# Expert calls in which heads 0 and 1 are routed before the first dot, and half of the first v rows is gathered behind the first 32 u

## The reference, cut to what matters

```python
q = (xc @ w_q).reshape(PEER_CHUNK, PEER_HEADS, 2, PEER_HALF)      # 128 tokens, 8 heads
s = jnp.einsum('thid,hikd->thik', q, sub_keys)
s1, i1 = lax.top_k(s[:, :, 0], 16); s2, i2 = lax.top_k(s[:, :, 1], 16)
# the 16 best of the 256 sums s1 + s2 name 16 of 16,384 experts per token and head
u = u_emb[eidx]
hid = jax.nn.gelu(jnp.einsum('td,thkd->thk', xc, u))
return jnp.einsum('thk,thkd->td', gate * hid, v_emb[eidx])
```

## Time and profile before

| | us |
|---|---|
| median of three runs | 3790.22 (3789.51 to 3791.14) |
| span of the profiled execution | 3786.1 |
| first gather of call 1, 2, 3 issued at | 582.9, 1480.4, 2606.9 |
| last gather issued in call 3 | 3287.4 |
| DVE busy in the span | 1978.6 (52%) |
| POOL busy | 1527.8 (40%) |
| PE busy | 3085.9 (82%) |

### The profile page before, as it was taken

How to read it: one execution, slowest core, us unless ns; L and a number is a source line. 1 busy time by engine, 2 the same in 40 slices (tenths; PEclk the granted TensorE clock), 3 DMA queues, 4 the chain that set the end, 5 groups by cost and what they waited for, 6 DMA issues and landing times.

```text
span 3786.1 us, 31001 instructions
## 1 busy us (share of the span) xinstructions
PE 3085.9 (82%) x11474; PEld 1349.7 (36%) x11474; DVE 1978.6 (52%) x4448; ACT 367.0 (10%) x923; POOL 1527.8 (40%) x1579
## 2 busy tenths in 40 slices
PE   7999887778988987688888889888466666798897
PEld 4484445233532325222222224446011111144343
DVE  0051447767776635666666623355777777223132
ACT  1000321110000001000000000131000000012111
POOL 0010004646665662666666641002677777500000
PEclk9999998879999988899999989999889898899999
DMA  6274137979999997999999987416999999942322
GB/s 270 99 292 169 72 128 300 358 252 392 410 408 410 405 385 273 362 412 411 411 412 412 412 344 281 171 68 261 371 409 409 409 407 397 361 164 82 113 89 100
DMA packets 257376, 1125.52 MB, mean 297 GB/s; under 512 B 29636, under 2 KB 34980, under 8 KB 238024
## 3 DMA queue, kind: packets, MB, share of 16 engines
q0 software_dynamic: 221184, 805.40, 54.1%
q1 hardware_dynamic: 32456, 312.82, 21.2%
q10 hardware_dynamic: 3584, 5.31, 0.4%
HBM read 1117.06 MB, written 6.37 MB: 297 GB/s over the span
## 4 chain that ended last, share of the span: by engine, by line
PE 44%; DMA 26%; DVE 17%; POOL 7%; issue 4%; ACT 3%; DVEq 0%; SPq 0%; ACTq 0%; POOLq 0%
DMA big<-in_u,xT 17%; PE ps L234 16%; DMA big<-in_v,xT 7%; POOL big L2132 7%; DVE big L2101 6%; PE ps L1961 5%; PE ps L1900 5%; PE ps L656 4%; PE ps L1399 2%; PE ps L670 1%; PE ps L1517 1%; PE ps L1435 1%; DVE small L910 1%; PE ps L387 1%; PE ps L587 1%
## 5 line engine op out<-in xcount | busy, mean ns | idle before, releaser
L1961 PE MATMUL ps<-big,bc 128*32 128x512 f32 x3072 | 1074.1, 671 | 344.1 <-DMA big<-in_v,xT 330.5
L2101 DVE CUSTOM_DVE_ANT_0 big<-big,ps 128x1024 f32<-128x1024 f32 x768 | 926.5, 1215 | 427.6 <-DMA big<-in_u,xT 423.8
L2132 POOL DMA_INDIRECT big<-in_u,xT x768 | 729.2, 950 | 611.9 <-issue 163.5
L2132 POOL DMA_INDIRECT big<-in_v,xT x768 | 727.8, 948 | 281.6 <-issue 187.1
L234 PE MATMUL ps<-w,xT 128*128 128x512 f32 x1408 | 615.0, 598 | 8.8 <-ACT xT L256 6.0
L1961 PEld LDWEIGHTS ps<-big,bc 128*32 128x32 f32 x3072 | 194.8, 116 | 1102.0 <-DMA big<-in_v,xT 733.6
L234 PEld LDWEIGHTS ps<-w,xT 128*128 128x128 f32 x1408 | 268.4, 192 | 346.6 <-issue 334.0
L524 POOL TENSOR_TENSOR small<-small 128x32 f32<-128x32 f32 (+1 forms) x8 | 33.2, 4154 | 374.4 <-DVE small L495 250.6
L1900 PE MATMUL ps<-tmp,w 128*128 128x256 f32 x768 | 172.5, 387 | 2.0 <-ACT tmp L256 2.0
L656 PE MATMUL ps<-w,xT 128*128 128x512 f32 x384 | 167.1, 594 | 1.7 <-ACT bb L755 0.9
L1900 PEld LDWEIGHTS ps<-tmp,w 128*128 128x128 f32 x768 | 148.7, 195 | 24.0 <-ACT tmp L256 3.2
(11 more groups left out here) (305 smaller groups left out, 2783.4 us busy)
## 6 DMA issues: line engine op xcount, KB each, us to landing
w<-in_w_in SPq DMA_DIRECT2D x58, 2048.0 KB, 9.2
bc<-in_w_mod SPq DMA_DIRECT2D x21, 2048.0 KB, 10.6
w<-in_w_conv SPq DMA_DIRECT2D x24, 1536.0 KB, 9.1
w<-in_peer_wq SPq DMA_DIRECT2D x12, 2048.0 KB, 9.3
w<-in_w_out SPq DMA_DIRECT2D x10, 2048.0 KB, 8.1
w<-in_conv_out_w SPq DMA_DIRECT2D x6, 2048.0 KB, 8.7
big<-in_u,xT POOLq DMA_INDIRECT x768, 10.5
big<-in_v,xT POOLq DMA_INDIRECT x768, 10.8
```

The lines of the kernel that those rows point to most:

```text
L1961: ins = pe.e.matmul(self.ps[32 * g:32 * g + 32, 2 + half, :], p["diag"][part % 2][:, 256 * g + 32 * m:256 * g + 32 * m + 32], p["ring"][:, ...
L2101: dve.inc(dve.e.tensor_tensor_reduce(out=row, in0=row, in1=p["xc"], scale=1.0, scalar=0.0, op0=ALU.mult, op1=ALU.add, accum_out=p["hid"][t ...
L2132: ins = pool.e.indirect_dma_start(p["ring"][:, slot, :], None, table, bass.IndirectOffsetOnAxis(index, 0))
```

## The change

The list becomes u0 to u31, v0 to v15 (positions 32 to 47), then eight times four u and two v (u32 to u35 at 48 to 51, v16, v17, u36 to u39, ...), which ends with u63 at position 93 and v31 at 95. From position 96 on it is as before. DVE routes steps 0 and 1 one after the other ahead of the first dot; PE makes the scores of step 1 behind query 3 and not behind query 5; ACT makes the exponential of step 1 behind query 7 and not behind query 15.

```diff
     def peer_order(self):
-        order = [("u", e) for e in range(PART)]
-        for part in range(PARTS):
+        order = [("u", e) for e in range(PART)] + [("v", e) for e in range(PART // 2)]
+        for i in range(0, PART // 2, 2):
+            order += [("u", PART + 2 * i + j) for j in range(4)]
+            order += [("v", PART // 2 + i + j) for j in range(2)]
+        for part in range(1, PARTS):
...
-        for i in range(2, 6):
+        for i in range(2, 4):
             query(i)
         scores(1)
-        for i in range(6, 16):
+        for i in range(4, 16):
             query(i)
...
-            if i == 3:
-                self.gate_exp_act(act, name, p, 0)
+            if i in (3, 7):
+                self.gate_exp_act(act, name, p, i // 4)
...
-                if e % TOPK == 11 and e // TOPK + 1 < STEPS:
+                if e % TOPK == 11 and 1 < e // TOPK + 1 < STEPS:
...
-        alone(self.route_dve(dve, l, name, p, 0))
+        for step in range(2):
+            alone(self.route_dve(dve, l, name, p, step))
...
-                routing = self.route_dve(dve, l, name, p, step + 1) if step + 1 < STEPS else iter(())
+                routing = self.route_dve(dve, l, name, p, step + 1) if 1 < step + 1 < STEPS else iter(())
```

## The result

The changed kernel takes 3803.8 us (median of 14 runs, 3795.5 to 3808.8), the kernel before 3793.0 on the same chip (14 runs). The ratio is 1.0026, 95% interval 1.0018 to 1.0034: 7 to 13 us slower. The forecast was 3788 (3776 to 3802), 2 us faster.

The account below looks back on a forecast made before the run. DMA was taken to set the pace in calls 2 and 3, DVE and the attention chain in call 1's part 1. Span 3786.1 + 10 - 2.3 - 10.2 = 3783.6, median 4.1 above: 3788 us, range 3776 to 3802.

Parts of the forecast that it names:

- Call 3: Third expert call: waits at u16 and u32 go, DMA keeps full rate without a hole; 10.2 us gained.
- the margin: Call 3 at u48: DMA has work until 2721.0, u48 lands at 2719.9 at the soonest; one us.
- Rival (c): All calls: each DMA hole closed at u32 opens at u48; 3790 + 0 to 5 us; 45% together with the forecast.
- Call 2: Second expert call: hole ahead of u32 closes, one of some 6 us opens ahead of u48; 2.3 us gained.
- the 5 named as the bound of being wrong: Call 2, dot 34: the forecast would be wrong if DVE waited there for less than 5 us.
- Call 1: First expert call, ten slots, attention beside: scores 3 come 22.3 us late, dot 63 9.5 us late; 10 us lost.
- what is left of DVE's idle time behind scores 3: Call 1 up to dot 63's end: idle time of 20.9 us shrinks to 9 to 11.
- rival (b): DVE's stall is the price: call 1 loses the whole 20 us, call 2 gains nothing; 3800 us; 25%.
- The 4.0 us for scores 3: Call 1: DVE's wait for scores 3 itself, counted as gone from the idle time.
- The sum: Whole kernel: 3786.1 + 10 - 2.3 - 10.2 = 3783.6 us for the span, 3787.7 for the median.
- The 4.1: Whole kernel: the median time lies 4.1 us above the span.
- (a): Early v pay in all calls, the stall at dot 34 hides; 3767 us in full, half of it 3777; 30%.

Follow-up runs that it names:

- scores3_first: Changed kernel with the four matmuls of scores 3 made ahead of part 0's first pair instead of behind eight pairs; ratio 1.0016, median 3799.8 us.
- pe_kept_busy: Changed kernel with three zero-adding PE matmuls at each place of u38 to u63 in call 1; ratio 1.0029, median 3803.9 us.
- side100: Changed kernel with the plan of call 1's work beside begun at position 100 instead of 16, on another chip; call 1 took 958.4 us.
- side_later: Changed kernel with the plan of call 1's work beside begun at position 25 instead of 16; ratio 1.0034.
- side100_v0: Changed kernel with the old list in call 1 and its work beside begun at position 100, on another chip; call 1 took 955.7 us.

## Why the prediction was wrong

**Call 3** (forecast: 10.2 us gained, no wait at u16 and u32, no hole): 8.8 gained. Right, but for a wait of 4.41 at u32 and one of 5.17 at u48 where the margin had been worked out as 1 us. Rival (c)'s mechanism was there and can have cost the missing 1 us, which is less than two traces of the same call differ by.

**Call 2** (2.3 gained, POOL waiting at u48, a hole near 1605): 2.9 gained. POOL waited 10.2 us for experts 3 at u48, 125.9 us behind the first gather where the forecast has experts 3 at 128.5. DVE waited 7.7 us at dot 34, over the 5 named as the bound of being wrong. DMA's share was 0.67 between 1630 and 1640, which is 1605 moved by the 26.5 us by which the call began later. Right.

**Call 1** (scores 3 at 109.8 behind the first gather, dot 63 9.5 us late, 10 us lost): scores 3 came at 107.5, so this step was right. The step that failed is the next one, what is left of DVE's idle time behind scores 3: "those for u rows (7.4) come down to perhaps 3 to 5, those for attention scores (6.4) to 2", "9 to 11 are left". The window from scores 3 to the end of dot 63 in the changed kernel, and DVE's waits in it:
```profile
693.20:784.05 90.85, 51.17 (x149) 20.25 (x148) 71.40 (x178) 13.64 (x49) 49.27 (x47) 0.66 0.80 289
...
DVE small L1811 <- PE ps L1740: 9.4, 4, 4.2
...
DVE big L2105 <- DMA big<-in_u,xT: 3.8, 2, 2.1
...
DVE small L1815 <- ACT w L1791: 2.2, 2, 1.1
```
DVE was busy for 71.4 us, as forecast (72). The waits for u rows (3.8) and for the exponential (2.2) came down as forecast. Those for attention scores (L1740), sized at 2, grew from 6.4 to 9.4. The idle time was 19.5 us of the 20.9 before, not 10: 9.5 more than forecast, less the 2.3 by which scores 3 came sooner and 0.6 of busy time, make about the 6.5 by which dot 63 missed the forecast (16.0 us late, not 9.5). Behind it comes what the forecast had at nothing: the last pair behind u63, which makes dot 64 23.5 us late, and the call 23.7. In call 1 this is rival (b), with a loss a little above its 20 us, given 25%; in call 2, where (b) has no gain, it is wrong.

One slip stands in the working. The 4.0 us for scores 3 are taken off the 20.9, but the window of the 20.9 begins at 670.4, when this wait was over. The list gives 7 to 9 us with it taken off and 11 to 13 without; the 10 lies between, so the slip isn't what missed. Of the two reasons behind the step, "there DVE and the chain through the attention set the pace, not DMA" came from a window of 95 us: in its first 70 DMA was full (0.98), in the last 25 its share was 0.75. And the waits were taken one by one as if each could shrink, when they were round trips: DVE waits for L1740, that stands behind a pair, that stands behind L1747, that waits for DVE. This chain is read from traces. What the runs show is that taking one wait away (scores3_first) left the call's length, that raising PE's clock (pe_kept_busy) left it too, and that the lateness shrank only where no work stood beside (side100, and call 3 with ten slots).

**The sum.** With what was measured, 3786.1 + 23.7 - 2.9 - 8.8 = 3798.1, and 4.1 more is 3802, near the median of 3803.8. The 4.1 hold for the three runs before the forecast, whose median was 3790.2; over 14 runs it is 3793.0, so 2.8 us of the miss against 3788 are the starting point. Two of three terms were right within 1.4 us; one was sized 10 instead of 24.

**The rivals.** (a) was right for call 3 alone. The rule of the Trainium skill behind it ("DMA: Bandwidth & Descriptors", section "Rules for kernel authors": issue early, wait late) agrees with call 3 with sixteen slots, where the list gave 4.0 us (7.2 without the routing ahead); with ten slots it gave -0.6 there, and call 1 was 21 to 27 us longer with the list (921.2 against 900.2, 924.4 against 897.5). Half of (a)'s 22.9 us gives 3779, not the 3777 of the prediction.

**Still open.** How the 24 us of call 1 divide between the ring at the head, the round trips with the work beside, and the last pair behind u63: with 8 v ahead hardly any is lost at the head (dot 48 2.2 us late) and still 13.4 at dot 64, so more than the ring is at work. Why 12 v cost as much as 16, and what held u32 in side_later, wasn't followed up.

## What to carry to other kernels

Before rows are fetched ahead, count the slots: a prefix that fills the ring ties the next needed row to the slowest consumer of the prefix. Idle time in a stretch with a second chain through the same queues may not be slack (here 19.5 of 20.9 us stayed); test it by moving the second chain away. Compare lists at their ends too: a pair moved from ahead of u62 to behind u63 went with 7 us between two dots. And cut the window before naming a bound: behind a mean DMA share of 0.92 stood 0.98 for the first 70 us and 0.75 for the rest.

## What the runs showed of the hardware

The granted clock rose when gaps were filled, and no time came of it here: three added matmuls at each of 26 rows, 11.8 us more of busy PE in 94.5 (64.34, before them 52.52), raised it from 0.65 to 0.80, and the stretch took 136.6 us instead of 137.1. The same kernel took 3793 to 3794 us on three chips and 3902 (3893 to 3915) on a fourth, 2.9% more, which is above any edit here; DMA moved 374 GB/s in a stretch of call 3 there (side100_v0) where the kernel before had 407.
